# Neighbourhood attention on strips of 16 columns with 256 local keys a unit, its bias added by VectorE in PSUM

## The reference, cut to what matters

```python
row_idx = jnp.clip(r - kr // 2, 0, rows - kr)[:, None] + jnp.arange(kr)[None, :]   # kr = rows = 8: all rows
col_start = jnp.clip(cq - NA_COLS // 2, 0, GRID_W - NA_COLS)                       # NA_COLS = 16, GRID_W = 64
col_valid = (cq[None, :] >= col_start[:, None]) & (cq[None, :] < col_start[:, None] + NA_COLS)
s_loc = jnp.einsum('brchd,brkwhd->bhrckw', qg, k_rows) * scale + bias[None]
s_loc = jnp.where(col_valid[:, None, :], s_loc, NEG_INF).reshape(b, h, rows, GRID_W, kr * GRID_W)
s_ctx = jnp.einsum('brchd,blhd->bhrcl', qg, kc) * scale
p = jax.nn.softmax(jnp.concatenate([s_loc, s_ctx], axis=-1), axis=-1)
```

## Time and profile before

| | before |
|---|---|
| median of the runs | 3508.9 us |
| the profiled execution's own time | 3505.03 us |
| its span (first to last instruction) | 3503.0 us |
| TensorE, VectorE, ScalarE, GpSimd busy | 87%, 28%, 24%, 19% |
| mean granted TensorE clock | 0.915 of full speed |
| neighbourhood attention, first score product to the merge's first product | 548.8 to 687.9 us |

### The profile page before, as it was taken

One profiled execution on the slowest core, in us unless ns is written; L12 is line 12 of the kernel. 1 busy time (PEld: TensorE's weight loads), 2 busy tenths in 40 slices (PEclk: granted clock), 3 DMA queues, 4 the chain that ended last, 5 costly groups with the idle time before them and its releaser, 6 DMA issues.

```text
span 3503.0 us, 37334 instructions
## 1 busy us (share of the span) xinstructions
PE 3057.5 (87%) x15444; PEld 2286.4 (65%) x15444; DVE 987.3 (28%) x1406; ACT 853.3 (24%) x1272; POOL 659.8 (19%) x348
## 2 busy tenths in 40 slices
PE   6888999999869899986758989999995948799997
PEld 3747886788733333325647668999995747487886
DVE  2232502411341111114253354121125063442113
ACT  4122422322300000003221233221123222243222
POOL 1201320044200000001100100622223201006443
PEclk8999999999889999998865989999997966899998
DMA  5143211022249999991310100121121100002222
GB/s 226 39 181 117 63 50 71 1 96 96 97 180 356 368 364 362 367 351 72 132 60 1 43 1 35 57 72 61 61 96 60 59 14 27 28 1 102 96 97 84
DMA packets 56492, 406.94 MB, mean 116 GB/s; under 512 B 6352, under 2 KB 6352, under 8 KB 9760
## 3 DMA queue, kind: packets, MB, share of 16 engines
q1 hardware_dynamic: 52416, 375.41, 28.5%
q0 software_dynamic: 3936, 29.48, 2.5%
HBM read 396.48 MB, written 8.39 MB: 116 GB/s over the span
## 4 chain that ended last, share of the span: by engine, by line
PE 78%; DVE 8%; DMA 7%; ACT 4%; issue 2%; POOL 1%; SPq 0%; DVEq 0%; POOLq 0%; ACTq 0%
PE psum L581 75%; DMA ring<-in_weights 7%; PE psum L584 3%; DVE arena L1672 1%; ACT hidden_high L1340 1%; ACT hidden L1334 1%; DVE arena L1730 1%; DVE arena L1734 0%; POOL arena L2434 0%; DVE arena L1731 0%; DVE arena L2219 0%; POOL weight_parts L2337 0%; ACT weight_parts L1304 0%; ACT hidden L1333 0%; DVE arena L2034 0%
## 5 line engine op out<-in xcount | busy, mean ns | idle before, releaser
L581 PE MATMUL psum<-hidden_high,weight_parts 128*128 128x384 f32 (+1 forms) x3296 | 868.5, 365 | 48.6 <-DVE hidden_low L1712 24.6
L2337 POOL TENSOR_TENSOR weight_parts<-ring,weight_parts 128x1024 fp32r<-128x1024 f32 x218 | 533.2, 2447 | 1689.8 <-ACT weight_parts L1304 1684.3
L581 PE MATMUL psum<-arena 128*128 128x64 f32 (+8 forms) x2992 | 656.6, 373 | 78.1 <-DVE arena L2200 32.4
L581 PEld LDWEIGHTS psum<-hidden_high,weight_parts 128*128 128x128 f32 x3296 | 611.9, 192 | 121.7 <-issue 32.9
L581 PEld LDWEIGHTS psum<-arena 128*128 128x128 f32 (+3 forms) x2992 | 437.0, 215 | 235.1 <-issue 202.1
L581 PE MATMUL psum<-hidden_low,weight_parts 128*128 128x384 f32 (+1 forms) x1648 | 519.8, 363 | 0.0
L1304 ACT ACTIVATE weight_parts<-ring 128x1024 fp32r<-128x1024 f32 x218 | 230.1, 1059 | 1090.1 <-PE psum L581 1089.5
L581 PE MATMUL psum<-ring,arena 128*64 128x512 f32 (+1 forms) x1560 | 382.3, 606 | 51.1 <-DMA ring<-in_weights 47.4
L581 PE MATMUL psum<-arena_parts,weight_parts 128*128 128x512 f32 (+1 forms) x1728 | 368.6, 373 | 12.9 <-DVE arena_parts L1834 12.9
L581 PEld LDWEIGHTS psum<-arena_parts,weight_parts 128*128 128x128 f32 x1728 | 317.9, 190 | 58.4 <-issue 14.3
L1349 ACT ACTIVATE arena<-psum 128x512 f32<-128x512 f32 (+4 forms) x234 | 166.5, 714 | 749.1 <-PE psum L581 510.0
(11 more groups left out here) (232 smaller groups left out, 2115.1 us busy)
## 6 DMA issues: line engine op xcount, KB each, us to landing
ring<-in_weights SPq DMA_DIRECT2D x356, 1024.0 KB, 5.9
saved_residual<-residual POOLq DMA_DIRECT2D x2, 3072.0 KB, 9.2
residual<-saved_residual POOLq DMA_DIRECT2D x2, 3072.0 KB, 11.0
arena<-in_rpb POOLq DMA_DIRECT2D x16, 224.0 KB, 8.4
residual<-in_acts POOLq DMA_DIRECT2D x1, 3072.0 KB, 19.2
arena<-in_t_count POOLq DMA_DIRECT2D x2, 1536.0 KB, 7.3
residual<-in_acts POOLq DMA_DIRECT2D x1, 2048.0 KB, 11.2
out_x<-residual SPq DMA_DIRECT2D x8, 256.0 KB, 2.0
```

Of the source, the lines that this page charges most:

```text
L581: return nc.tensor.matmul(o, lhsT, rhs, start=start, stop=stop)
L2337: G_.tensor_tensor(parts[:, i % 2, 1, :], ring[:, at:at + 1024], parts[:, i % 2, 0, :], ALU.subtract).then_inc(*E.sig("tile_split"))
```

## The change

The tokens of the image are put in the order of columns: position 8c + r for column c and row r. A unit's 128 queries are then a strip of 16 columns by 8 rows, and the window of a strip lies in two key tiles of 128 (16 columns each), if the tiles are cut at columns 8, 24, 40 and 56; the fourth tile is made of columns 56 to 63 and 0 to 7. So a unit has 256 local keys and 256 context keys: 512, four key tiles.

Queries and keys are put in that order by ScalarE as it copies them out of PSUM, with an output step of 8 elements. Values have tokens on partitions, so they are written to HBM by 16 DMAs and read back by one, all issued by ScalarE; `v_n` is projected first for that, ahead of `q_n` and `k_n`. The outputs are put back by VectorE's collecting copy. The bias tables, mask included, are built on the host, three tables of 256 columns for each of 8 heads, loaded by one DMA, and VectorE adds one to the scores in PSUM ahead of the maximum. The permutation constant, the 16 DMAs and GpSimd's eight adds go. `k_n` is projected in chunks of 256 and 512 tokens in place of two of 384.

```diff
@@ stream_plan
+    out += rhs("w_in", (0,), "v_n", B1["v_n"], 512)
     out += cols("w_in", (0,), "q_n", B1["q_n"], 4) + cols("w_in", (0,), "k_n", B1["k_n"], 4)
-    out += rhs("w_in", (0,), "v_n", B1["v_n"], 512)
@@ new constants and tables
+GRID_ROWS, GRID_COLS = 8, 64
+IMG_CHUNKS = ((0, CTX), (CTX, SEQ))
+COL_TILES = {5: np.r_[56:64, 0:8], 2: np.arange(8, 24), 3: np.arange(24, 40), 4: np.arange(40, 56)}
+COL_PAIRS = ((5, 2), (2, 3), (3, 4), (4, 5))
+def column_bias(rpb):
...
+    for i in (0, 1, 3):
+        q_col, row = 16 * i + n // GRID_ROWS, n % GRID_ROWS
+        start = np.clip(q_col - 8, 0, GRID_COLS - 16)[:, None]
+        for tile in COL_PAIRS[i]:
...
@@ spans
+            if name == "na":
+                return 2 * P, [*COL_PAIRS[qi], 0, 1]
+        def by_columns(ap):
+            return ap.rearrange("p (c r) -> p r c", r=GRID_ROWS)
+        def by_rows(ap):
+            return ap.rearrange("p (r c) -> p r c", r=GRID_ROWS)
@@ TensorE
+            project_tokens([("v_n", i) for i in range(4)], ("v_n",))
             for t in range(4):
                 project_tile(("q_n", t), ("q_n", t), IMG)
             for t in range(4):
-                project_tile(("k_n", t), ("k_n", t), ALL)
-            project_tokens([("v_n", i) for i in range(4)], ("v_n",))
+                project_tile(("k_n", t), ("k_n", t), IMG_CHUNKS)
...
-            pe.wait_ge(*E.next("bias_ready", 8))
+            pe.wait_ge(*E.next("values_by_columns", 16))
...
-                a0 = 6 - 2 * qi
-                return [(ps[:, 0:512], q, k[:, CTX:TOK], True, False),
-                        (ps[:, 0:512], C("flip"), nB[:, 2 * t + hh, a0 * 64:(a0 + 8) * 64], False, True),
-                        (ps[:, 512:768], q, k[:, 0:CTX], True, True)]
+                a, b = COL_PAIRS[qi]
+                if b == a + 1:
+                    r = [(ps[:, 256:512], q, k[:, a * P:(b + 1) * P], True, True)]
+                else:
+                    r = [(ps[:, 256:384], q, k[:, a * P:(a + 1) * P], True, True),
+                         (ps[:, 384:512], q, k[:, b * P:(b + 1) * P], True, True)]
+                return r + [(ps[:, 512:768], q, k[:, 0:CTX], True, True)]
@@ ScalarE
+            token_evac(("v_n",), nV)
+            act.wait_ge(*E.own())
+            far, near = dram["values"][0:448, :], dram["values"][448:SEQ, :]
+            for r in range(GRID_ROWS):
+                p0 = (r % 2) * 64
+                for to, c0, c1 in ((far, 8, 64), (near, 0, 8)):
+                    act.dma_start(to.rearrange("(c r) n -> r c n", r=GRID_ROWS)[r, :, :],
+                                  nV[p0 + c0:p0 + c1, 2 + r // 2, :]).then_inc(sem("values_saved"), 16)
             for t in range(4):
                 high()
...
-                act_(nQ[0:64, t, :], ps[0:64, 0:SEQ], ACT.Copy, scale=0.125)
+                act_(by_columns(nQ[0:64, t, :]), by_rows(ps[0:64, 0:SEQ]), ACT.Copy, scale=0.125)
...
+            act.wait_ge(*E.next("values_saved", 16 * 2 * GRID_ROWS))
+            act.dma_start(nV[:, 2:TT, :], dram["values"].rearrange("(a p) n -> p a n", p=P))\
+                .then_inc(sem("values_by_columns"), 16)
             for t in range(4):
-                evac(("k_n", t), tok_view(nK[:, t, :], ALL), ALL, ahead=True)
-            token_evac(("v_n",), nV)
+                high()
...
+                act_(nK[:, t, 0:CTX], ps[:, 0:CTX], ACT.Copy)
+                act_(by_columns(nK[:, t, CTX:CTX + 448]), by_rows(ps[:, 512:1024])[:, :, 8:64], ACT.Copy)
+                act_(by_columns(nK[:, t, CTX + 448:TOK]), by_rows(ps[:, 512:1024])[:, :, 0:8], ACT.Copy)\
+                    .then_inc(*E.read("k_n", t))
@@ VectorE, maxes and collect
+                    if name == "na":
+                        table = (0, 1, 1, 2)[qi] * 2 * P
+                        tt_(ps[:, 256:512], ps[:, 256:512], nB[:, 2 * t + hh, table:table + 2 * P], ALU.add)\
+                            .then_inc(*E.sig("bias_added"))
+                        dve.wait_ge(*E.own())
                     ins = V.reduce_max(nm, ps[:, 512 - L:768], AXX, negate=True)
...
+                    if name == "na":
+                        to, of = by_rows(to), by_columns(of)
+                    V.tensor_copy(to, of).then_inc(*E.read("O", name, t))
@@ GpSimd
-            pool.dma_start(nMask, dram["t_colmask"]).then_inc(sem("mask_loaded"), 16)
-            for h in range(8):
-                for half in range(2):
...
-                    pool.dma_start(nB[64 * half:64 * half + 64, h, :].rearrange("p (a c) -> p a c", a=14), src)\
-                        .then_inc(sem("bias_loaded"), 16)
...
-            for h in range(8):
-                b = nB[:, h, :].rearrange("p (a c) -> p a c", a=14)
-                G_.tensor_tensor(b, b, nMask.unsqueeze(1).to_broadcast([P, 14, 64]), ALU.add)\
-                    .then_inc(*E.sig("bias_ready"))
+            pool.dma_start(nB, split(dram["bias"], h=8)).then_inc(sem("bias_loaded"), 16)
```

More of the change, by code:

```diff
@@ L215, in constants @@
     u = np.arange(DW)[None, :] - 640 - q[:, None]
[L216 to L219, removed]
     inv_count = np.zeros((4, TOK), f)
@@ L229, in constants @@
         "t_mla": np.concatenate([cm, sm], 1).astype(f),
-        "t_colmask": colmask.astype(f),
         "t_count": np.broadcast_to(inv_count.reshape(1, -1), (P, 4 * TOK)).astype(f),
     }
+GRID_ROWS, GRID_COLS = 8, 64
[3 more added lines that the diff above has]
+def column_bias(rpb):
+    n = np.arange(P)
+    padded = np.concatenate([rpb.reshape(rpb.shape[0], -1), np.full((rpb.shape[0], 1), -1e30, np.float32)], 1)
+    tables = []
+    for i in (0, 1, 3):
+        q_col, row = 16 * i + n // GRID_ROWS, n % GRID_ROWS
+        start = np.clip(q_col - 8, 0, GRID_COLS - 16)[:, None]
+        for tile in COL_PAIRS[i]:
+            k_col = COL_TILES[tile][n // GRID_ROWS][None, :]
+            at = (row[None, :] - row[:, None] + 7) * 31 + (k_col - q_col[:, None] + 15)
+            at = np.where((k_col >= start) & (k_col < start + 16), at, padded.shape[1] - 1)
+            tables.append(padded[:, at])
+    return np.stack(tables, 1).transpose(2, 0, 1, 3).reshape(P, -1)
 def program(nc, dram, scratch, out):
@@ L433, in program @@
         AT2 = NA + 8192
-        nB = split(area(NA + 12288, 7168), h=8)
-        nMask = area(NA + 19456, 64)
+        nB = split(area(NA + 12288, 6144), h=8)
         nQb = split(YC, a=4)
@@ L1466, in _ @@
                 ps = cols("q_n", t)
-                act_(nQ[0:64, t, :], ps[0:64, 0:SEQ], ACT.Copy, scale=0.125)
-                act_(nQb[64:128, t, :], ps[64:128, 0:SEQ], ACT.Copy, scale=0.125).then_inc(*E.read("q_n", t))
-            for t in range(4):
-                evac(("k_n", t), tok_view(nK[:, t, :], ALL), ALL, ahead=True)
-            token_evac(("v_n",), nV)
+                act_(by_columns(nQ[0:64, t, :]), by_rows(ps[0:64, 0:SEQ]), ACT.Copy, scale=0.125)
+                act_(by_columns(nQb[64:128, t, :]), by_rows(ps[64:128, 0:SEQ]), ACT.Copy, scale=0.125)\
+                    .then_inc(*E.read("q_n", t))
+            act.wait_ge(*E.next("values_saved", 16 * 2 * GRID_ROWS))
+            act.dma_start(nV[:, 2:TT, :], dram["values"].rearrange("(a p) n -> p a n", p=P))\
+                .then_inc(sem("values_by_columns"), 16)
+            for t in range(4):
+                high()
+                act.wait_ge(*E.written("k_n", t))
+                ps = cols("k_n", t)
+                act_(nK[:, t, 0:CTX], ps[:, 0:CTX], ACT.Copy)
+                act_(by_columns(nK[:, t, CTX:CTX + 448]), by_rows(ps[:, 512:1024])[:, :, 8:64], ACT.Copy)
+                act_(by_columns(nK[:, t, CTX + 448:TOK]), by_rows(ps[:, 512:1024])[:, :, 0:8], ACT.Copy)\
+                    .then_inc(*E.read("k_n", t))
             modulation_rows(("mod2", 0), 1)
@@ L1953, in _ @@
             modulation_add(("mod2", 0), 1, modB[0], "bmod20")
+            dve.wait_ge(*E.next("bias_loaded", 16))
             attention("na", attn_area(AT2), split(YC, a=4), 0)
@@ L2544 @@
         "router": x["w_router"][0].reshape(KT, P, NE).transpose(1, 0, 2),
-        "rpb": np.pad(x["na_rpb"][0], ((0, 0), (0, 0), (48, 48))),
+        "bias": column_bias(x["na_rpb"][0]),
         **constants(),
@@ L2552 @@
     out = nc.dram_tensor("out_x", (P, KT, SEQ), f32, kind="ExternalOutput").ap()
+    dram["values"] = nc.dram_tensor("neighbourhood_values", (SEQ, 512), f32, kind="Internal").ap()
     scratch = nc.dram_tensor("saved_residual", (P, KT, TOK), f32, kind="Internal").ap()
```

10 lines of the change are left out of this document (2 added, 8 removed).

## The result

| | before | changed |
|---|---|---|
| median, runs of one comparison | 3508.15 us (3499.76 to 3508.94, 4 runs) | 3453.86 us (3450.18 to 3457.24, 4 runs) |
| ratio to before | | 0.985, 95% interval 0.983 to 0.9869 |
| the profiled execution's own time | 3505.03 us | 3450.18 us |
| its span | 3503.0 us | 3448.3 us |
| neighbourhood attention, first score product to the merge's first product | 548.83 to 687.93, 139.10 us | 548.74 to 630.70, 81.96 us |

The change makes the kernel 54.3 us faster by the medians; 57 were forecast (3452 against 3453.9, inside the forecast's own 3447 to 3456). In the changed kernel the helper `mm` is line 604, `flip` 607, the addition in PSUM 1799, the maximum 1802, the exponential 1397.

The account below looks back on a forecast made before the run. TensorE's own work was taken to bound the kernel. 3505.0 - 58.0 (stage) + 1.0 (projections) = 3448.0 profiled, 3452 as median; forecast 3447 to 3456 at chance 0.63, range 3446 to 3464.

Parts of the forecast that it names:

- The unit: Neighbourhood attention loop: 2.25 us a unit against 4.15, from TensorE work of 2.19 and a chain of 2.24.
- second delay: Odd units: ScalarE copies transposed probabilities after the next exponential, ending at 2.73 when TensorE wants it at 2.68; 0.05 late.
- Start, turns, end: Neighbourhood stage around its 30 units: start 6.2 us, three turns 2.7 in all, end 4.7.
- The projections: `v_n`, `q_n`, `k_n` up to the modulation sums: 93.2 us against 92.2, so 1.0 us lost.
- Steps costed at nothing: Sixteen DMAs on ScalarE, write and read-back, stepped copies, bias load and GpSimd's removed additions: hidden, 0 us.
- cover: ScalarE's DMAs ahead of the third `q_n` tile: its split ends at 13.1, TensorE needs it at 15.0; 1.9 us slack.
- Rival 1: Stage loop bound by the chain through VectorE: 2.5 us a unit, +7.5, 3459 to 3460; chance 0.22 together with rival 2.
- theory B: Experiments' version of VectorE's chain binding the loop: whatever is put on or taken off VectorE counts in full, every unit.
- Rival 2: Projections: DMAs on ScalarE at GpSimd's price, or 256-column chunks at the price of 384, +5.2, 3457; chance 0.22 with rival 1.
- Rival 3: Stage: products of 256 columns or the gaps give back a large part, 3470 to 3505; chance 0.04.
- Rival 4: Stage: TensorE at half clock throughout because of the gap in each unit, 149 us against 139.1, 3520; chance 0.02.
- Downstream: After the stage: nothing takes the gain back, since SyncE waits for TensorE up to 186.5 us and the ring is full.

Follow-up runs that it names:

- e4: Changed kernel with VectorE's addition left out, so attention is computed without bias and mask; 3445.19 us, ratio 0.9832.
- e3: Changed kernel with a second, unused VectorE maximum of 256 columns in each unit; 3459.97 us, ratio 0.9866.
- e1: Changed kernel with the bias added by TensorE as a product of 256 columns instead of VectorE's addition; 3464.42 us, ratio 0.9889.
- e6: Changed kernel with ScalarE copying the first slot of values out ahead of the fourth weight split, in all four value projections; 3447.18 us, ratio 0.983.
- c1: Changed kernel run again, unchanged, in another comparison; 3453.88 us, ratio 0.9844.
- e9: e8 with the sixteen DMAs in four groups behind the `q_n` tiles' copies and the reading back behind the first `k_n` tile; 3426.18 us, ratio 0.9776.
- e8: Changed kernel with e6's earlier copy and TensorE waiting for each value slot only when writing to it; 3425.18 us, ratio 0.9771.
- e5: Changed kernel with values projected last again, after `q_n` and `k_n`, their DMAs moved along; 3463.59 us, ratio 0.9881.

## Why the prediction was right, step by step

**The unit.** Forecast 2.25 us, measured 2.29. TensorE's work was forecast at 2.19; e4, where nothing else is on the chain, shows 2.20. The chain from the end of the scores to the transposes was forecast at 2.24 and took 2.31. The timeline of one unit of the changed kernel (start us, us, engine line op; in brackets the idle time before):

```profile
564.09 0.60 PE L607 MATMUL psum<-consts_sb,arena 128*128 128x128 f32 x4
564.29 0.43 DVE L1799 TENSOR_TENSOR psum<-psum,arena 128x256 f32<-128x256 f32 x1 [0.62 <-PE psum L604]
...
564.75 0.69 DVE L1802 TENSOR_REDUCE small<-psum 128x1 f32<-128x512 f32 x1
565.48 0.69 ACT L1397 ACTIVATE arena<-psum,small 128x512 f32<-128x512 f32 x1 [1.60 <-DVE small L1802]
...
566.40 0.63 PE L607 MATMUL psum<-consts_sb,arena 128*128 128x128 f32 x4
```

0.20 until VectorE starts, 0.46 for addition and self-wait (forecast 0.48), 0.73 for the maximum and handover (0.74; the forecast's 0.05 each for self-wait and handover, and the bound of 0.3, were estimates of the author that no row gives; the changed kernel shows 0.46 - 0.43 = 0.03 and 0.73 - 0.69 = 0.04), then 566.40 - 565.48 = 0.92 where 0.82 was read off the window attention. That last term, exponential to transposes, was 0.1 too small; it is all that was mis-sized in the chain. Half of what the chain is longer than TensorE's work is paid, by e3: (2.31 - 2.20) / 2 = 0.06, and 0.09 is measured. The prediction's second delay, ScalarE's copy for odd units, was put at 0.05 and shows as 0.03: the value products start 566.87 - 566.40 = 0.47 after the transposes there, and 564.52 - 564.09 = 0.43 in the even unit. Half of both is 0.07; the remaining 0.02 a unit stays open.

**Start, turns, end.** Start 555.09 - 548.74 = 6.35 us (forecast 6.2), end 630.70 - 625.92 = 4.78 (4.7). Between them lie 70.83 us; less 30 x 2.29 = 68.7 they leave 2.1. A turn adds 578.82 - 573.41 - 2 x 2.29 = 0.83, 2.5 for the three (forecast 2.7), and the last two units, with no more scores to make, take 0.3 less than two others (forecast: nothing). The forecast put 0.47 of waiting at each turn; the chain decides where it said (the piece at 575.64), but TensorE's last work ahead of it starts at 576.90 and takes 0.44, so that 577.67 - 577.34 = 0.33 is waited. The stage came to 81.96 us against 81.1, the gain to 57.1 against 58.0, and the merge began at 630.70 ("near 631").

**The projections** are the step that failed in size: +1.0 was forecast, +3.35 measured. Of the 2.35 more, 1.6 is `v_n`: 34.33 against 32.7, at a clock of 0.59 in its first 3.7 us. The prediction named this ("up to 2 more; it isn't counted"). Of six traces with the same wait of 0.94 us ahead of `v_n`, four (e1, e3, e4, e6) show the clock at 1.00 in the first 3.7 us, and 32.9 us where `v_n` is a piece of its own, and two (the changed kernel at 0.59, 34.33 us; c1 at 0.50, 35.71) do not. So about a third of its price belonged into the sum. The wait ahead of it took 0.94 against 0.7 (+0.2), the wait after it 2.19 against 2.2, `q_n` with `k_n` and the first sums 58.06 against 57.6 (+0.5). e9 has the same products at full clock throughout: 88.90 - 32.7 = 56.2, again 0.5 more than the 55.7 of before. So this 0.5 is left for the keys in chunks of 256 and 512, which were put at nothing with bounds of -0.9 and +5.2. The reason given there, that 128 columns look bound by the weight load, agrees with the trace of before: from 316 to 332 us TensorE's weight loads are busy for 16.00 of 16.00 us.

**Steps costed at nothing.** The sixteen DMAs took 6.32 us of ScalarE's queue (changed kernel, timeline):

```profile
483.54 6.32 ACTq L1495 DMA_DIRECT2D neighbourhood_values<-arena  x16
489.96 1.06 ACT L1330 ACTIVATE weight_parts<-ring 128x1024 fp32r<-128x1024 f32 x1 [6.45 <-PE psum L604]
490.93 1.15 ACT L1501 ACTIVATE arena<-psum 64x512 f32<-64x512 f32 x1
```

That is 0.395 each with the gap to the next, not 0.333: 1.0 us more of the 1.9 of cover. In this trace they stayed hidden; in c1, where the clock stayed up, 0.94 us showed. The prediction's cover for them counted with a lower clock after the wait; it was 0.58 here (482 to 485) and 1.00 in c1 (485.2 to 489). ScalarE's copies of 64 x 512 with a step of 8 take a mean of 1.17 us, twice the 0.59 of the same copies before, but below the three times that would have mattered. The bias load and GpSimd's removed additions cost and gave nothing that can be seen (the window attention is 0.7 us shorter, of which 0.5 also lies between two traces of the kernel before).

**The rivals.** Rival 1, VectorE's chain as the bound: its price for addition and self-wait, 0.99, was 0.46, and theory B fell in e3. Rival 2: the place was right and the price small, 0 to 0.94 us as the kernel stands. Rival 3: a product of 256 columns costs half one of 512, as e1's unit shows (0.43 us more, beside 0.86). Rival 4, half the clock throughout the stage: the row of 560 to 624 shows 1.00. What the records have of idle time there, 0.48 us in all, lies at the three turns (TensorE's ends are modelled, so that the 0.1 in each pair of units doesn't show), and the changed kernel is a weak test; e3, with a gap in every pair of units and 4.7 us of idle time, is the stronger one and shows 1.00 too. That a gap in each unit would hold the clock at half was a supposition of the author; no run shows it.

**Downstream** nothing gave the gain back: SyncE still waits for TensorE up to 189.8 us at a time (186.5 before), and what follows the stage took 2817.6 us against 2815.1.

**How much of the agreement is luck.** The mechanism was right: each term is found where it was said to be. The total is nearer than the terms are. The stage gained 0.9 us less and the projections lost 2.35 more than forecast, and in the profiled execution what lies ahead of the projections and behind the stage made up 0.9 of that. The medians agree to 1.9 us, while four runs of the changed kernel lie 7 us apart.

## What to carry to other kernels

Work out TensorE's own work and the longest chain through the other engines for the same loop, from rows: here, where they were about equal (2.31 and 2.20 us), the 0.46 us of addition and self-wait on VectorE cost 0.09 a unit in the loop, 0.43 at the stage's start and 0.29 at each turn (the changed kernel beside e4). Cutting the work itself (512 local keys to 256) brought 47.6 us and moving the bias 23.2 or 9.6 depending on what had been cut first, because the cut also halves the product that is moved: parts of a change are not to be added up. After a stage is cheap, the short waits between stages come next: two small edits around the projections gave 29 us more, half of what the change had brought. A wait that is taken away can uncover the next one, as e6 and e8 show at the third `q_n` tile (1.90 and 1.96 us), and cover that is counted at a low clock can be gone when the clock stays up, as c1 shows (clock 1.00, a wait of 0.94 us).

## What the runs showed of the hardware that was not expected

- A wait of 0.94 us on TensorE (with waits of 2.0 and 0.8 us in the 6 us ahead of it) was followed by a granted clock of 0.59, of 0.50 and 0.71, or of 1.00 in different traces of the same code ahead of it: `v_n` took 34.33, 35.71 or 32.9 us. After the wait of 2.2 us behind `v_n` it was 0.58 (482 to 485) in the changed kernel and 1.00 (485.2 to 489) in c1, after the 1.96 us in e8 0.60 (485.2 to 489). No run here shows what decides.
- A ScalarE copy of 64x512 out of PSUM took 0.59 us before and a mean of 1.17 with an output step of 8 elements. VectorE's collecting copy, which reads PSUM with a step of 8, took 0.692 us, as it did for 512 columns without a step in the window attention.
- A DMA issued by ScalarE occupied its queue for 0.395 us with the gap to the next (16 in 6.32; one alone has a median of 0.324 and at most 0.780), where one of SyncE's takes 0.333 and of GpSimd's 0.786. In e5 the last of sixteen writes landed 9.4 us after its issue; the reading back of 1 MB landed 5.5 us after its own there, and 8.3 in the changed kernel.
